# One core, a two-block network: four waits of TensorE laid on smaller pieces

## The reference

```
h = rms_norm(x, norm_pre_mix[l])
proj = h @ w_in                                   # 1024 -> 3592
aq, ak = apply_rope(...), apply_rope(...)         # 8 heads of 64
attn_out = dilated_attention(aq, ak, av)          # softmax under three patterns
qkv = silu(causal_dwconv(dn_qkv, dn_conv_w))      # 3 x 512 channels, 4 taps
o = gated_delta_rule(dq, dk, dv, beta, g)         # 4 heads, K = V = 128
dn_out = rms_norm(o, dn_norm_w) * silu(z)
mix = concat([attn_out, dn_out]) @ w_out
x = x + rms_norm(mix, ...);  x = x + rms_norm(conv_glu_ffn(rms_norm(x, ...)), ...)
```

```
v_new = u_i - w_i @ state
o = q_i @ state + qk_i @ v_new
state = state * gl + k_i^T @ v_new
```

## Time and profile before

| | |
|---|---|
| median of 3 runs | 1928.96 us (1923.92 to 1930.76) |
| the profiled execution | 1936.42 us, its span 1934.6 us |
| PE busy | 1678.4 us, 87% of the span |
| DVE, ACT, POOL busy | 872.2, 546.1, 572.2 us |
| granted TensorE clock, mean | 0.945 of full |

### The profile page before, as it was taken

How to read it: one execution, slowest core, us unless ns; L and a number is a source line. 1 busy time by engine, 2 the same in 40 slices (tenths; PEclk the granted TensorE clock), 3 DMA queues, 4 the chain that set the end, 5 groups by cost and what they waited for, 6 DMA issues and landing times.

```text
span 1934.6 us, 19045 instructions
## 1 busy us (share of the span) xinstructions
PE 1678.4 (87%) x6306; PEld 1022.7 (53%) x6306; DVE 872.2 (45%) x2136; ACT 546.1 (28%) x1521; POOL 572.2 (30%) x597
## 2 busy tenths in 40 slices
PE   7998988787778877677696999899999999999998
PEld 2545563444434322222242587687775587677775
DVE  1477666655546365646444246332123246322112
ACT  2234324323232323233332235321112135221111
POOL 0000046655564666676664002110000002110000
PEclk9999999988888988899898999999999999999999
DMA  9745169988997999999999331074543331074510
GB/s 355 265 174 206 50 236 393 337 314 323 336 330 278 354 365 360 360 382 407 363 372 376 133 131 44 5 267 160 166 142 109 131 115 60 1 272 134 173 64 22
DMA packets 171255, 438.54 MB, mean 227 GB/s; under 512 B 12291, under 2 KB 58531, under 8 KB 171028
## 3 DMA queue, kind: packets, MB, share of 16 engines
q0 software_dynamic: 81824, 299.99, 41.5%
q1 hardware_dynamic: 89334, 137.33, 20.2%
HBM read 436.23 MB, written 1.05 MB: 226 GB/s over the span
## 4 chain that ended last, share of the span: by engine, by line
PE 56%; issue 32%; DVE 4%; ACT 3%; DMA 2%; another core or an unknown queue 1%; DVEq 1%; SPq 0%; POOL 0%; ACTq 0%
PE psum L1107 14%; PE psum L1118 6%; PE psum L881 4%; PE psum L822 2%; PE psum L791 2%; PE psum L1128 2%; PE psum L792 2%; PE psum L630 2%; PE psum L610 2%; PE psum L805 2%; PE psum L1096 2%; PE psum L1078 1%; PE psum L910 1%; PE psum L513 1%
## 5 line engine op out<-in xcount | busy, mean ns | idle before, releaser
L791 PE MATMUL psum<-arena 128*128 128x512 f32 x512 | 298.7, 668 | 165.5 <-ACT arena L1495 85.7
L2095 DVE CUSTOM_DVE_ANT_0 arena<-arena,psum 128x1024 f32<-128x1024 f32 x224 | 273.6, 1221 | 305.1 <-DMA arena<-in_expert_u,indices 211.9
L1234 POOL DMA_INDIRECT arena<-in_expert_v,indices x256 | 245.6, 959 | 203.1 <-PE psum L792 87.3
L792 PE MATMUL psum<-arena 128*128 128x512 f32 x512 | 282.8, 636 | 0.0
L1107 PE MATMUL psum<-activations_T,weight_ring 128*128 128x256 f32 x1280 | 279.2, 379 | 0.0
L1231 POOL DMA_INDIRECT arena<-in_expert_u,indices x256 | 244.6, 955 | 90.9 <-issue 77.2
L791 PEld LDWEIGHTS psum<-arena 128*128 128x128 f32 x512 | 96.2, 206 | 325.0 <-issue 197.4
L1107 PEld LDWEIGHTS psum<-activations_T,weight_ring 128*128 128x128 f32 x1280 | 243.0, 190 | 39.8 <-issue 7.7
L2327 DVE SCALAR_TENSOR_TENSOR arena<-psum,small,arena 128x254 f32<-128x254 f32 (+1 forms) x176 | 76.8, 478 | 322.2 <-ACT arena L1641 318.6
L1186 POOL TENSOR_TENSOR small<-small 128x1 f32<-128x1 f32 (+4 forms) x29 | 30.5, 1050 | 560.3 <-DVE small L2206 218.0
L792 PEld LDWEIGHTS psum<-arena 128*128 128x128 f32 x512 | 105.5, 206 | 139.1 <-issue 139.1
(11 more groups left out here) (396 smaller groups left out, 2062.9 us busy)
## 6 DMA issues: line engine op xcount, KB each, us to landing
weight_ring<-in_ffn_w_in SPq DMA_DIRECT2D x44, 1024.0 KB, 7.8
weight_ring<-in_w_in SPq DMA_DIRECT2D x15, 2048.0 KB, 12.8
weight_ring<-in_w_ada SPq DMA_DIRECT2D x12, 2048.0 KB, 7.8
arena<-in_ffn_w_out POOLq DMA_DIRECT2D x22, 1024.0 KB, 5.2
weight_ring<-in_w_out SPq DMA_DIRECT2D x6, 2048.0 KB
weight_ring<-in_w_pq SPq DMA_DIRECT2D x4, 2048.0 KB, 10.2
weight_ring<-in_w_in SPq DMA_DIRECT2D x2, 2080.0 KB
arena<-in_expert_u,indices POOLq DMA_INDIRECT x256
```

The costliest lines, as they stand in the source:

```text
L791: mm(o0, DIAG[:, n % ND, :], VROWS[n % NV][:, 0:512], start=m == 0, stop=m == PICKS - 1)
L792: mm(o1, DIAG[:, n % ND, :], VROWS[n % NV][:, 512:1024], start=m == 0, stop=m == PICKS - 1).then_inc(sem("v_used"), 1)
L1234: nc.gpsimd.indirect_dma_start(VROWS[g % NV], None, a["expert_v"], bass.IndirectOffsetOnAxis(ap=where, axis=0)).then_inc(sem(f"v_row{g % N ...
L2095: ttr(out=DOTJ[n >= UNIT], in0=UROWS[n % NU], in1=h2, scale=1.0, scalar=0.0, op0=ALU.mult, op1=ALU.add, accum_out=DOT[:, i, m:m + 1]).then ...
```

## The change

Four edits, all in the second block; no instruction changes its engine.

1. **Queries turned during the keys' rotation.** VectorE now counts up `rot2` twice per layer, after the queries and after the keys of tile 1. TensorE waits for the first count ahead of the queries' transposes and for the second ahead of the keys'.
2. **Column transposes behind their own SiLU piece.** TensorE waits for two, four and six pieces ahead of the q, k and v columns instead of for six ahead of all.
3. **The delta rule's state in pairs of heads.** Each d bank of the chain holds two heads; VectorE's copies and the subtraction are done for 256 columns each. The wait of the output of chunk 0 on the subtraction is gone.
4. **Values by 256 columns.** In `attend()`, the two heads of a pair go through one product whose moving side and output are 2 x 128 columns: 3 products where 6 stood.

```diff
@@ -848,18 +848,18 @@
                         h -= 2
                         pe.wait_ge(a_free, turned[h])
                         o = bank_d()
-                        for e in range(2):
-                            for i in range(2):
-                                for s in range(i + 1):
-                                    ins = mm(o[:, e * SEQ + i * P:e * SEQ + (i + 1) * P], V2[:, s, h * P:(h + 1) * P], EPT[:, h % 2, e, i + s, :], start=s == 0, stop=s == i)
+                        both = o.rearrange("p (e i q) -> p e i q", e=2, i=2)
+                        for i in range(2):
+                            for s in range(i + 1):
+                                ins = mm(both[:, :, i, :], V2[:, s, h * P:(h + 1) * P], EPT[:, h % 2, :, i + s, :], start=s == 0, stop=s == i)
                         ins.then_inc(d_full, 1)
 
                 if L:
                     w = weights(512)
                     values(0, w)
 
-                pe.wait_ge(sem("rot2"), L + 1)
                 for wh in range(2):
+                    pe.wait_ge(sem("rot2"), 2 * L + wh + 1)
                     for g in range(2):
                         o = bank_a()
                         for q in range(4):
@@ -894,9 +894,9 @@
                 ins.then_inc(a_full, 1)
                 m["ba"] = c["a"]
 
-                pe.wait_ge(sem("cv_silu"), 6 * (L + 1))
                 m["tq"] = []
                 for wh in range(3):
+                    pe.wait_ge(sem("cv_silu"), 6 * L + 2 * wh + 2)
                     for i in range(2):
                         o = bank_a()
                         for h in range(DH):
@@ -1022,29 +1022,33 @@
                 pe.wait_ge(d_free, c["d"])
                 pe.wait_ge(sem("vb_ready"), L + 1)
                 pe.wait_ge(sem("qkd_ready"), L + 1)
-                o = bank_d()
-                for h in range(DH):
-                    ins = mm(o[:, h * P:(h + 1) * P], TU[:, h, :], TQ[:, 2, 0, h * P:(h + 1) * P], start=True, stop=True)
-                ins.then_inc(d_full, 1)
-                pe.wait_ge(d_free, c["d"])
-                o = bank_d()
-                for h in range(DH):
-                    ins = mm(o[:, h * P:(h + 1) * P], AT[:, 2, h, :], UU[:, 0, h * P:(h + 1) * P], start=True, stop=True)
-                ins.then_inc(d_full, 1)
-                pe.wait_ge(d_free, c["d"])
+                def pair(g, stationary, moving):
+
+                    o = bank_d()
+                    for q in range(2):
+                        h = 2 * g + q
+                        ins = mm(o[:, q * P:(q + 1) * P], stationary[:, h, :], moving[:, h * P:(h + 1) * P], start=True, stop=True)
+                    ins.then_inc(d_full, 1)
+                    return c["d"]
+
+                first_done = [pair(g, TU[:, 0:4, :], TQ[:, 2, 0, :]) for g in range(2)]
+                carried = []
+                for g in range(2):
+                    pe.wait_ge(d_free, first_done[g])
+                    carried.append(pair(g, AT[:, 2, :, :], UU[:, 0, :]))
                 o = bank_a()
                 for h in range(DH):
                     ins = mm(o[:, h * P:(h + 1) * P], QKDT[:, h, 0, :], UU[:, 0, h * P:(h + 1) * P], start=True, stop=True)
                 ins.then_inc(a_full, 1)
                 m["o"] = [c["a"]]
-                pe.wait_ge(d_free, c["d"])
-                o = bank_d()
-                for h in range(DH):
-                    ins = mm(o[:, h * P:(h + 1) * P], TU[:, 4 + h, :], TQ[:, 2, 1, h * P:(h + 1) * P], start=True, stop=True)
-                ins.then_inc(d_full, 1)
-                pe.wait_ge(d_free, c["d"])
+                second_done = []
+                for g in range(2):
+                    pe.wait_ge(d_free, carried[g])
+                    second_done.append(pair(g, TU[:, 4:8, :], TQ[:, 2, 1, :]))
                 o = bank_a()
                 for h in range(DH):
+                    if h % 2 == 0:
+                        pe.wait_ge(d_free, second_done[h // 2])
                     mm(o[:, h * P:(h + 1) * P], QKDT[:, h, 1, :], UU[:, 0, h * P:(h + 1) * P], start=True, stop=False)
                     ins = mm(o[:, h * P:(h + 1) * P], QKDT[:, h, 2, :], UU[:, 1, h * P:(h + 1) * P], start=False, stop=True)
                 ins.then_inc(a_full, 1)
@@ -2127,7 +2131,8 @@
                         tt(q.rearrange("p (h e) -> p h e", h=AH), o.rearrange("p h f e -> p h (f e)"), bcast(rope2[:, 0, i, :], 1, [P, AH, AD]), ALU.mult).then_inc(d_free, 1)
                         dve.drain()
                         ins = tt(q, q, RTMP[:, wh, :], ALU.add)
-                ins.then_inc(sem("rot2"), 1)
+                        if i == 1:
+                            ins.then_inc(sem("rot2"), 1)
                 step, early = iter(range(ATT_STEPS)), iter(range(PAIRS))
 
                 def probabilities():
@@ -2281,12 +2286,16 @@
                         dve.drain().then_inc(sem("qkd_ready"), 1)
                     if 0 < lv < 6:
                         dve.drain()
-                o = full()
-                copy(UU[:, 0, :], o).then_inc(d_free, 1)
-                o = full()
-                tt(TQ[:, 2, 1, :], TQ[:, 2, 1, :], o, ALU.subtract).then_inc(d_free, 1)
-                o = full()
-                copy(UU[:, 1, :], o).then_inc(d_free, 1)
+                pairs = [slice(g * 2 * P, (g + 1) * 2 * P) for g in range(2)]
+                for e in pairs:
+                    o = full()
+                    copy(UU[:, 0, e], o[:, 0:2 * P]).then_inc(d_free, 1)
+                for e in pairs:
+                    o = full()
+                    tt(TQ[:, 2, 1, e], TQ[:, 2, 1, e], o[:, 0:2 * P], ALU.subtract).then_inc(d_free, 1)
+                for e in pairs:
+                    o = full()
+                    copy(UU[:, 1, e], o[:, 0:2 * P]).then_inc(d_free, 1)
                 for i in range(2):
                     n = m["o"][i]
                     rsqrt_of_mean([(4 * i, 4 * i + 4, P)])
```

## The result

| | before | changed |
|---|---|---|
| median of 22 runs each | 1928.74 us (1922.16 to 1936.34) | 1921.79 us (1908.11 to 1928.4) |
| ratio | 1 | 0.9957, 95% interval 0.9943 to 0.9971 |
| span of the profiled execution | 1934.6 us | 1921.0 us |

A forecast was written before the change was run, and what follows sets the result against it. TensorE is the spine of the second block, and its waits, with half clock at or behind them, bound the kernel. Terms of 2.2 + 3.8 + 4.3 + 0.15 = 10.4 us off 1928.96 gave 1918.5 us, range 1912 to 1926.

The forecast's parts named there:

- the rotation's wait: TensorE's idle stretch in layer 0's rotation, 2.23 us, would shrink to about 1.4 us with eight transposes moved into it.
- both rivals of structure: Pairs in the state's chain do not overlap, 1921.4 us, chance 0.08; strided value products are slow, 1925.4 us, chance 0.06.
- two halves of a copy: In the state's chain, two 256-column copies would cost VectorE 0.1 us more than the whole copy.
- edit 3, chain: State's chain: 2.1 us gained in each layer, and 0.9 for the clock of layer 1.
- edit 3, gap behind it: Between chunk 1's end and the output projection: new idle of 1.3 and 0.65 us may bring low clock, costing 0.8 us.
- the clock's part of edit 1: Behind layer 0's rotation: the clock holds with chance 0.8, worth 1.65 us, so 0.8 x 1.65 of the 2.2.
- a low stretch ... one chance in four: Behind the gap after the state's chain, in each layer: half clock costing up to 1.7 us, 0.8 in all.
- The gates' term: From gate columns to z product: 3.8 us gained, 2.1 in layer 0 and 1.7 in layer 1, bounds 2.0 and 5.1.
- likely to go: Layer 0's second half-clock stretch, behind the SiLU wait of 1.21 us, would vanish without that wait; term 2.1 us.
- the pairs do not overlap: State's chain: the second pair waits for the first, chain gains only 0.7 us a layer; 1921.4 us, chance 0.08.
- the clock gives nothing: Rotation, SiLU stretch and chain: waits shrink but low stretches stay in number; gain 6.4 us, 1922.5 us, chance 0.21.
- bar of 0.5%: Whole kernel: what a measurement can tell from no change, 9.6 us, or below 1919.3 us.

The follow-up runs named there:

- x3: Only the state in pairs of heads, against the kernel before; executed once: chain 8.83 and 8.84 us, where before had 11.01 and 12.29.
- x4: Only the values by 256 columns, against the kernel before; executed once: 62.46 us from tile 1's values to the gate columns instead of 62.55.
- x1: Only the queries turned during the keys' rotation, against the kernel before; executed once: rotation 17.16 us, where before had 19.36.
- x10: The kernel before once more, unchanged; executed once: rotation 18.04 us, chain 11.01 us in both layers.
- x2: Only the column transposes behind their own SiLU piece, against the kernel before; executed once: gates 7.23 and 7.90 us, where before had 10.15 and 9.65.
- x7: The changed kernel with idle identity products in the gap behind the state's chain: ratio to before 0.9951 (0.9937 to 0.9964).
- x9: The changed kernel once more, unchanged: ratio to before 0.9958 (0.9935 to 0.9981).
- x11: The changed kernel with the wait of chunk 0's output on the subtraction put back; executed once: chain 9.62 and 9.61 us, against 8.84.
- x6: The changed kernel with gate columns computed by 128 columns per product instead of 8: ratio to before 0.9943 (0.9930 to 0.9957).
- x8: The changed kernel with 128-column gate products and idle products behind the chain and ahead of L822 and L1100: ratio to before 0.9928 (0.9915 to 0.9942).
- x12: The changed kernel with 128-column gate products and idle products only in the gap behind the chain: ratio to before 0.9934 (0.9911 to 0.9956).
- x5: The kernel before with gate columns computed by 128 columns per product instead of 8: ratio to before 0.9994 (0.9983 to 1.0005).

## Why the prediction was right, and where it was not

The lengths at full clock were right to 0.1 us: the rotation's wait of 1.36 us (1.4), the chain of 8.84 (8.9), the gates of 7.23 (working from the 8-column products' end, 1.65 us behind the last piece), 0.09 us a layer for the values. No edit had to be taken back, and both rivals of structure fell: the pairs overlap (x3) and strided operands cost nothing (x4). One length was off without effect: two halves of a copy took 0.87 us where the whole had taken 0.69, so 0.18 more instead of 0.1, and the pairs' overlap hid it.

What was wrong is the clock, and with it the sum. With the profiles of kernels alike in one place put together, a mean for each term (few stretches each, and from groups that differ ahead of the block, so these are estimates):

| term | forecast | from all profiles | how |
|---|---|---|---|
| edit 1 | 2.2 | 1.4 | 0.88, and 1.68 in 2 of 6 profiles without the edit (before, x3; 1.3 and 0.5 of it fall inside the rotation's length, the rest into the values), 0 of 8 with it |
| edit 2 | 3.8 | 3.8 | gates without it 10.23 / 10.15 (before, x1, x3, x4, x10), with it 8.57 / 8.05 (changed, x2, x7, x9, x11) |
| edit 3, chain | 5.1 | 4.8 | 11.22 in the mean over 12 chains, 8.84 now |
| edit 3, gap behind it | -0.8 | -1.4 | 1.7 us in 4 of 10 (changed, x3, x6, x9, x11), 0 of 12 without the edit, 0 of 6 with fillers |
| turn of the layers | 0 | -1.3 | 1.7 us in 4 of 7 kernels with edit 3 and no filler there, 0 of 6 without; and 0.33 |
| edit 4 | 0.15 | 0.2 | 62.55 to 62.46 twice |
| sum | 10.4 | 7.5 | |

The sum of 7.5 us is near the measured 8.3 and inside its interval. All steps that failed erred the same way, and the measured time lies in the range because the range was wide: it holds every gain from 3 to 17 us.

Three steps failed. First, the clock's part of edit 1 was read from the one profile of before. The clock fell behind the rotation in 2 of 6 profiles without the edit, not each time, so 1.3 us of the 2.2 should have been near 0.5 (and that it never fell in the 8 profiles with the edit would come about by chance one time in six). I said that the terms hold as means over positions, and had taken a single position's cost as such a mean. Second, "a low stretch ... one chance in four" behind the chain was too low: it was 4 in 10. The edit moved idle time as much as it removed some: three stops of 0.8 us with products between them became one gap of 1.15 and 0.67, and low stretches, seen inside the chain before (2 of 12 chains, none of 16 now), were seen behind it. That the gap is the cause is likely but not shown: with fillers in it the low stretch is absent in both layers of x7, x8 and x12, but it was absent in 6 of the 10 layers without fillers too, in both of x6 and x11 among them. Were fillers without effect, all four low stretches would miss the six filled gaps about one time in nine. Third, the turn of the layers was in no term.

This last one is only partly settled. In all eight kernels with edit 3 VectorE stands for 0.42 us between two tiny operations on tile 1's norm, with nothing named that it waits for. In the seven without a filler there TensorE therefore waits 2.14 us instead of 1.84 ahead of L822. TensorE's rows, before and after:

```profile
1490.16 13.97 PE L822 MATMUL psum<-weight_ring,activations_T 128*128 128x512 f32 x32 [1.84 <-DVE arena L2343]
```

```profile
1480.06 15.67 PE L822 MATMUL psum<-weight_ring,activations_T 128*128 128x512 f32 x32 [2.14 <-DVE arena L2352]
```

The timelines of VectorE, before and after:

```profile
1488.27 0.15 DVE L2020 TENSOR_SCALAR small<-small 128x1 f32<-128x1 f32 x1 [4.47 <-ACT arena L1608]
1488.51 0.16 DVE L2022 SCALAR_TENSOR_TENSOR small<-small 128x1 f32<-128x1 f32 x1
```

```profile
1477.88 0.15 DVE L2024 TENSOR_SCALAR small<-small 128x1 f32<-128x1 f32 x1 [4.47 <-ACT arena L1612]
1478.45 0.16 DVE L2026 SCALAR_TENSOR_TENSOR small<-small 128x1 f32<-128x1 f32 x1 [0.42 <-issue]
```

TensorE's 2.1 us are in all seven kernels with edit 3 and no filler there, 1.8 in all six without the edit; the low stretch follows in 4 of the 7. The stop of 0.42 us seems to belong to a place in VectorE's stream, not to what edit 3 computes. Counted over all its records, drains and semaphore steps too, VectorE stops with no named cause for 0.43 us ahead of record 2112 and for 0.56 ahead of record 2241 in all fourteen profiles. A third such stop is ahead of record 2497 in the eight with edit 3, and ahead of record 2880, far behind in layer 1, in the six without. Edit 3 adds three instructions a layer, so the tiny operation, number 2494 before, becomes number 2497; before, number 2497 was a drain beneath an operation of 0.68 us. Why VectorE stops at such places no run shows. Nor does any tell whether the 0.3 us more of idle time bring the low clock. 4 of 7 against 0 of 6 is little, and all four are in profiles of the slower kind (changed, x9, x11, x12), none in the other three (x3, x6, x7), so what sets the groups apart may matter as much.

The gates' term was right in sum by luck: it was forecast as 2.1 us in layer 0 and 1.7 in layer 1 and came out as 1.7 and 2.1. I expected the second low stretch of layer 0 to be "likely to go"; both stayed in the changed kernel's profile, in x7 and in x9, and in x2 and x11 fewer came. What brings them: with narrow products and without the wait for the last piece there is at least one in nine of ten stretches (all but layer 0 of x2), with wide products and without that wait none in six (x6 and x8 in one group, x12 in the other). With wide products and the wait there is one in two (x5).

By the median alone the wrong rivals look best: "the pairs do not overlap" (1921.4) and "the clock gives nothing" (1922.5) lie nearest to 1921.79. The first is refuted by the chain of 8.84 us. The second came near by another way: not because the low stretches at the waits stayed in number, but because new ones came where the change made or left gaps. The bar of 0.5% for telling a change was set too high as well: the medians differ by 7 us, less than its 9.6, and the interval of the ratio still excludes 1.

## What to carry to other kernels

Splitting a chain between two engines into halves paid here what the sum of durations says, and one wait that was not needed was worth a third of it. Where low stretches of the clock come and go between executions, price an edit from several of them: one profile shows only where they happened to lie. And count the idle time that an edit gathers in one place, not only what it removes. Products made wider at the same pace kept the clock up at no cost in all six stretches; idle products in the gap cost nothing either, and whether they keep the clock up needs more executions than these.

## What the runs showed of the hardware

A product of 8 columns and one of 128 started 0.11 us apart alike (L893: 3.63 and 3.73 us for 32 records), but only behind the narrow ones did the clock fall while TensorE was busy without a break. The low stretches in the block lasted 3.4 us each, sometimes two in a row. Their number and places can change from one execution of the same kernel to the next (x10 against the first profile of before), and can come back almost whole (x9: the same five and one more).
